# One decoder layer with product-key experts: looking up the chosen experts in two passes over packed payloads instead of three, and letting GpSimd split 16 table blocks first instead of 12

## What is computed

```
v1, i1 = lax.top_k(s1, K)          # 16 of 128 keys, first half of the query
v2, i2 = lax.top_k(s2, K)          # 16 of 128 keys, second half
cand = (v1[..., :, None] + v2[..., None, :]).reshape(TB, PEER_HEADS, K * K)
sc, ci = lax.top_k(cand, K)
idx = (jnp.take_along_axis(i1, ci // K, axis=-1) * PEER_N_KEYS
       + jnp.take_along_axis(i2, ci % K, axis=-1))
gate = jax.nn.softmax(sc.astype(jnp.float32), axis=-1)
act = jax.nn.gelu(jnp.einsum('thed,td->the', u_table[idx], xb).astype(jnp.float32), approximate=False)
return jnp.einsum('the,thed->td', (gate * act).astype(xb.dtype), v_table[idx])
```

## Time and profile before

| | us |
|---|---|
| median of 3 runs | 1542.87 |
| the profiled execution, its own time | 1549.56 |
| its span, first to last instruction | 1547.5 |
| PE busy | 1483.3 (96%) |
| DVE busy | 1184.3 (77%) |
| POOL busy | 674.9 (44%) |
| ACT busy | 641.2 (41%) |

### The profile page before, as it was taken

How to read it: one execution, slowest core, us unless ns; L and a number is a source line. 1 busy time by engine, 2 the same in 40 slices (tenths; PEclk the granted TensorE clock), 3 DMA queues, 4 the chain that set the end, 5 groups by cost and what they waited for, 6 DMA issues and landing times.

```text
span 1547.5 us, 23496 instructions
## 1 busy us (share of the span) xinstructions
PE 1483.3 (96%) x8069; PEld 1318.8 (85%) x8069; DVE 1184.3 (77%) x2357; ACT 641.2 (41%) x1058; POOL 674.9 (44%) x385
## 2 busy tenths in 40 slices
PE   6999889899999999999999999789999999999999
PEld 6879658788989998999999999768888888888887
DVE  4527473288999999878998899647787787787886
ACT  5363452222423433347777776332332322423321
POOL 2223141133558578864545544124334344343341
PEclk9999989999999999999999999989999999999999
DMA  5400202221559989999999999989999999999993
GB/s 200 143 28 1 109 1 72 82 82 59 169 201 325 332 286 309 381 370 341 351 361 367 358 378 372 365 299 351 354 352 349 347 354 349 351 345 348 354 348 124
DMA packets 186648, 412.68 MB, mean 267 GB/s; under 512 B 12980, under 2 KB 112564, under 8 KB 185048
## 3 DMA queue, kind: packets, MB, share of 16 engines
q1 hardware_dynamic: 144984, 260.87, 48.0%
q0 software_dynamic: 41600, 151.03, 25.9%
HBM read 361.37 MB, written 50.46 MB: 266 GB/s over the span
## 4 chain that ended last, share of the span: by engine, by line
PE 56%; DVE 25%; DMA 12%; issue 3%; POOL 3%; ACT 1%; SPq 1%; DVEq 0%; ACTq 0%
PE banks L1736 15%; PE banks L2011 11%; PE banks L2012 11%; PE banks L2013 11%; DMA u_rows<-in_u,idx 8%; DVE u_rows L1538 4%; DVE u_lo L1521 3%; DVE gate_rows L1593 3%; DMA u_raw<-in_uT 2%; DVE picked L1491 2%; POOL u_lo L715 2%; DVE picked L1486 2%; DVE e_f L1494 2%; PE banks L1943 1%; DVE oh L1589 1%
## 5 line engine op out<-in xcount | busy, mean ns | idle before, releaser
L763 POOL DMA_INDIRECT v_rows<-in_v,idx x128 | 202.8, 1584 | 341.7 <-DVE x_res L1673 295.9
L2011 PE MATMUL banks<-v_hi,w_hi 128*128 128x512 f32 x768 | 300.1, 391 | 7.2 <-DVE v_lo L1615 7.2
L2012 PE MATMUL banks<-v_lo,w_hi 128*128 128x512 f32 x768 | 299.9, 390 | 0.0
L2013 PE MATMUL banks<-v_hi,w_lo 128*128 128x512 f32 x768 | 299.7, 390 | 0.0
L731 POOL DMA_INDIRECT u_rows<-in_u,idx x160 | 205.4, 1284 | 154.0 <-DVE z L1538 108.1
L1088 ACT ACTIVATE v_hi<-v_raw 128x1024 fp32r<-128x1024 f32 x128 | 125.8, 1049 | 340.1 <-PE banks L2013 321.5
L1615 DVE TENSOR_TENSOR v_lo<-v_raw,v_hi 128x1024 fp32r<-128x1024 f32 x128 | 153.5, 1220 | 125.4 <-ACT v_hi L1088 125.4
L1943 PE MATMUL banks<-h_hi,u_lo 128*128 128x352 f32 x1024 | 189.9, 328 | 18.3 <-DVE u_lo L1521 11.4
L1943 PE MATMUL banks<-h_lo,u_hi 128*128 128x352 f32 x1024 | 198.2, 328 | 0.0
L715 POOL TENSOR_TENSOR u_lo<-u_raw,u_hi 128x1024 fp32r<-128x1024 f32 x64 | 159.4, 2493 | 84.1 <-DVE opened L1558 53.9
L1943 PE MATMUL banks<-h_hi,u_hi 128*128 128x352 f32 x1024 | 192.2, 330 | 3.2 <-ACT act_out L1012 3.2
(11 more groups left out here) (268 smaller groups left out, 2040.6 us busy)
## 6 DMA issues: line engine op xcount, KB each, us to landing
u_raw<-in_uT SPq DMA_DIRECT2D x128, 512.0 KB, 6.1
v_raw<-in_v SPq DMA_DIRECT2D x128, 512.0 KB, 6.0
gates<-gate_scratch SPq DMA_DIRECT2D x32, 768.0 KB, 12.4
act_scratch<-act_out SPq DMA_DIRECT2D x128, 176.0 KB, 4.6
gate_scratch<-stage SPq DMA_DIRECT2D x11, 2048.0 KB, 8.7
act_in<-act_scratch SPq DMA_DIRECT2D x32, 704.0 KB, 7.0
wi_raw<-in_w_in SPq DMA_DIRECT2D x8, 1024.0 KB, 8.6
wq_raw<-in_w_q SPq DMA_DIRECT2D x8, 1024.0 KB, 5.4
```

What stands on the lines that cost most here:

```text
L763: nc.gpsimd.indirect_dma_start(v_rows[s % V_ROWS][:], None, v_flat, bass.IndirectOffsetOnAxis(ap=idx0[:, s:s + 1], axis=0)).then_inc(vg_in ...
L2011: mm(y, w, v_hi[q][:, j, ds], start=first and j == 0, stop=False)
L2012: mm(y, w, v_lo[q][:, j, ds], start=False, stop=False)
L2013: end = mm(y, w_lo[q][:, j, t * P:(t + 1) * P], v_hi[q][:, j, ds], start=False, stop=last and j == GROUP - 1)
```

## The change

- **Two passes instead of three.** `pay` now carries the position too: before the layout, `PACK` = 32768 times the position at which the pair will stand is added to the two parts of the payload (one more DVE instruction of 256 elements in each `choose`, with a wait behind it), from a constant of 32 columns. The position found is multiplied by `PACK` when it is cast. The first pass subtracts the two, over the same 3200 elements; at the winner the difference is the expert's number, below 16384, elsewhere it is at least 16384 away from zero. The second pass takes the minimum of the absolute values. The copy `iota_c` (L1447) goes.
- **GpSimd splits 16 blocks first.** `POOL_FIRST` is 16, `SHARE_FROM` 20: POOL splits blocks 0 to 15 ahead of its gathers, DVE 16 to 19, and then they alternate.
- **Dots.** The "aa" at n = 14 and 16 go, since they stand two blocks ahead of POOL's shared blocks; four "a" come at n = 58, 62, 66 and 70. The number of dots in the lookup stage stays 71, that of all 160, and the gate stage's dots stay where they were.
- **Pieces.** `PIECE_SIZE` is 1800, the sizes follow the new pieces (25,100 for each `choose` instead of 31,400), and at each block the pieces are run ahead of `splits_and_dots(n)`, not behind it. They begin at n = 14 instead of n = 10.

```
-POOL_FIRST, SHARE_FROM = 12, 16
+POOL_FIRST, SHARE_FROM = 16, 20
...
-for _n in range(PRE + 32, POST):
+for _n in [*range(PRE - 14, PRE, 4), *range(PRE + 32, POST)]:
     DOTS[_n] += "a"
...
-PIECE_SIZE = 2150
-CHOOSE_SIZES = (400, 2000, 1000, 3100, 1000, 1900, 600, 3350, 3350, 3350, 3350, 3350, 3350, 200, 400, 700)
+PIECE_SIZE = 1800
+CHOOSE_SIZES = (400, 2400, 1000, 3100, 1000, 1900, 600, 3350, 3350, 3350, 3350, 200, 400, 700)
...
-            step(nc.vector.tensor_copy(iota_c[:], consts[:, C_IOTA:C_IOTA + CAND]))
...
+                settle()
+                step(nc.vector.tensor_tensor(pay_f[:], pay_f[:], bc(packed_at, 2, PH), ALU.add))
                 settle()
...
-                step(nc.vector.tensor_copy(sc_f[:], sc_i[:]))
+                step(nc.vector.tensor_scalar(sc_f[:], sc_i[:], PACK, None, ALU.mult))
...
-                    step(nc.vector.tensor_tensor(
-                        picked[:], bc(sc_f[:, hs, :], 3, CAND),
-                        bc(bc(iota_c[:], 1, TOPK), 1, PH // 2), ALU.is_equal))
+                    step(nc.vector.tensor_tensor(picked[:], bc(pay[:, hs, :], 2, TOPK), bc(sc_f[:, hs, :], 3, CAND),
+                                                 ALU.subtract))
                     yield
                     settle()
-                    step(nc.vector.tensor_tensor(picked[:], picked[:], bc(pay[:, hs, :], 2, TOPK), ALU.mult))
-                    yield
-                    settle()
-                    step(nc.vector.reduce_sum(e_f[:, hs, :], picked[:], axis=AX_X))
+                    step(nc.vector.tensor_reduce(e_f[:, hs, :], picked[:], AX_X, ALU.min,
+                                                 apply_absolute_value=True))
...
             for n in range(POOL_FIRST - 2, PRE):
-                splits_and_dots(n)
                 while done < (n - POOL_FIRST + 3) * PIECE_SIZE:
                     done += next(sizes)
                     next(work, None)
+                splits_and_dots(n)
...
+    first = np.array([at0 + (a - a0) * n for a0, na, n, at0 in RUNS for a in range(a0, a0 + na)])
+    at_pair = (PACK * np.concatenate([first, np.arange(TOPK)])).astype(np.float32)
```

More of the change, by code:

```diff
@@ L61 @@
 C_ID, C_IOTA, C_MIN, C_NEG, C_FREQ, C_GQ, C_GK = 0, 128, 256, 384, 512, 544, 736
-C_W = 928
+C_OFF = 928
+C_W = 960
+PACK = float(2**15)
 V_ATT, V_ML, V_CQ, V_CKV, V_BI, V_BF = 0, 8, 12, 14, 15, 16
@@ L208, in build @@
         gk = consts[:, C_GK:C_GK + DQK]
+        packed_at = consts[:, C_OFF:C_OFF + 2 * TOPK].rearrange("p (s a) -> p s a", s=2)
         c_raw = at("c_raw", 22, [P, KD, NW])
@@ L285, in build @@
         cand_tmp = at("cand_tmp", 95, [P, PH, CAND])
-        iota_c = at("iota_c", 96.75, [P, CAND])
         sc_i = at("sc_i", 97.5, [P, PH, TOPK], U32)
@@ L300, in build @@
         idx1 = at("idx1", 19.875, [P, NE], I32)
-        z1 = at("z1", 19.625, [P, NE])
+        z1 = at("z1", 203, [P, NE])
         z1t = at("z1t", 103.125, [P, NE])
@@ L2051 @@
         np.broadcast_to(inv_freq.astype(np.float32), (P, HALF)),
-        rows(q_norm_g), rows(k_norm_g)], axis=1)
+        rows(q_norm_g), rows(k_norm_g), rows(at_pair)], axis=1)
     head_rows = np.zeros((H, H, P), np.float32)
```

## The result

The changed kernel has a median of 1527.75 us (1522.25 to 1542.04, 15 runs), the one before 1542.87 us (1538.47 to 1547.04, 15 runs); the ratio is 0.9899 with a 95% interval of 0.988 to 0.9918, so it is faster by 1.0%, 15 to 16 us. 1529 was forecast. The sum behind that number held less well than the number, as the stages show: between the two profiled executions the gain is 1549.56 - 1528.92 = 20.6 us, where the sum has 14.25. The changed kernel's profiled execution took 1528.92 us.

A forecast was written before the change was run, and what follows sets the result against it. PE bounds the kernel, losing 21.4 us in the lookup stage to a late DVE, a full DVE, then full DMA engines. Terms -6.6 - 7.65 - 0 = -14.25 on the median 1542.87 give 1528.6, say 1529 us; range 1524 to 1538.

The forecast's parts named there:

- The start: `choose(0)` and block 12: shorter `choose(0)` and POOL's 16 first splits remove PE's wait and slow matmuls, -6.6 us.
- DVE from 459.6 to 627.25: Lookup stage: relieved DVE wins back 7.65 of 11.85 us, leaving 3 for uneven loading and 1.2 for the `idx1n` halt.
- What gets out of the way: In `choose`: eight long two-input passes go, freeing POOL at up to eight places by 3.1 us; no own term.
- The last 16 blocks: Lookup stage from 627.25 to 691.0 us: four more gathers offset by the old debt; 2.95 us lost stays.
- The debt: Last 16 blocks before: one to three late gathers caught up in 25 us, set against four gathers' 5.0 us.
- The gate stage, unchanged: Behind the lookup stage: dots and one-hot rows do not change, the stage moves whole, 5.76 us a block.
- The signs named beforehand: Changed profile: no wait at block 12, first gather 445 to 448, minimum 3.4 to 3.6, lookup end about 677 us.
- The sum onto the median: Whole kernel: the gain of 14.25 us, put on the median of 1542.87, gives 1528.6, say 1529 us.
- A: Lookup stage from block 47 on: DMA engines take over, losing 12 us; gain 8, 1535 us; chance 0.26.
- B: Lookup stage: DVE's lead and POOL's relief swallow the rest; residue 3 us, gain 18.4, 1524.5 us; chance 0.13.
- C: In `choose`: absolute minimum costs 6.95 us, only the start is won; gain 5 to 8, 1536 to 1538; chance 0.08.
- D: In `choose`: absolute minimum dear, a reduction of 9.6 us; kernel slower, 1551 us and more; chance 0.03.

The follow-up runs named there:

- e1: Changed kernel's two passes alone, with first splits, dots and order of pieces of the kernel before; 1524.19 us, ratio 0.9872 to the kernel before.
- e2: Kernel before, three passes kept, with the rest of the change (16 first splits, moved dots, pieces ahead of splits); 1541.25 us, ratio 0.999 to before.
- e5: Changed kernel with the absolute minimum done twice, as a piece of its own; 1531.65 us, ratio 0.9921 to the kernel before.
- e6: Changed kernel with the subtraction done twice and the minimum once; 1541.93 us, ratio 0.9983 to the kernel before.
- e11: Changed kernel run again unaltered, in the third group of runs; 1527.09 us, ratio 0.9891 to the kernel before.
- e3: Changed kernel run again unaltered, in the first group, for a second profile; 1523.36 us, ratio 0.9875 to the kernel before.
- e8: Changed kernel with all sixteen single dots of the gate stage moved into the lookup stage; 1533.99 us, ratio 0.9933 to the kernel before.
- e9: Changed kernel with four of the gate stage's single dots moved to lookup blocks 21, 27, 33, 39; 1524.0 us, ratio 0.9878 to the kernel before.
- e10: Changed kernel with eight gate-stage dots moved to lookup blocks 21 to 42, a repeat run; 1525.13 us, ratio 0.9882 to the kernel before.
- e12: The kernel of e1 with eight gate-stage dots moved to lookup blocks 21 to 42; 1530.52 us, ratio 0.9905 to the kernel before.

## Why the prediction was right, and which terms were mis-sized

*The start, -6.6 us: right.* 6.6 us in one profile of before and 5.5 in the other became 0.0. What was put down to GpSimd's 16 first splits needs only the shorter `choose(0)` (e1), and they alone do not shorten the run by more than its noise (e2).

*DVE from 459.6 to 627.25, 4.2 us left: mis-sized, 0.0 is left.* The relief was priced rightly: minimum 3478 ns, and subtraction 4028 ns, six of them at 24.2 us, the dear end of the stated 20.9 to 24.2. The packing add, 0.45 us in the sum, shows in e1 as

```profile
439.47 0.43 DVE L1455 TENSOR_TENSOR pay_f<-pay_f,consts 128x256 f32<-128x256 f32 x1
```

What was wrong is the 3 us left for uneven loading and the 1.2 for the `idx1n` halt. The halt is still there, 3.8 us in DMA, and PE does not feel it. The reason given for the loss was too simple as well: a DVE without idle time was called the cause, while PE's waits there name GpSimd's `u_lo` (6.9 us) and hardly DVE's (0.8 us), and a DVE just as full in e5 leaves PE at pace until block 55.

*What gets out of the way, no term: the term was missing.* GpSimd's lateness was taken as part of DVE's losses. With as many long passes on DVE (e5, e6) the form of the third pass is worth 10 us. The working had the row for it, a gather's issue of 4.03 us against 0.94, and the changed page shows it summed up: 160 issues fell from 205.4 to 189.8 us. The Trainium skill's page "SBUF — State Buffer", section "Who interferes with whom", says that on this chip a `tensor_reduce` never contends with GpSimd, and the runs agree: with a second minimum (e5) the mean issue is 1440 ns, in the changed kernel over the same stretch 1449. The same section's inference, that writing descriptors is not held up by a two-input `tensor_tensor`, does not carry over to the whole issue of a gather, which is held up in e6. Which part of the issue it is, the descriptors or another, no run tells.

*The last 16 blocks, 2.95 us left: mis-sized.* 1.0 is left, and that is PE's own work. The second profile of before shows the same 1.0, so the loss that was left standing was that execution's. The debt that was set against the four gathers was also overrated: 25 us are 6.6 blocks at PE's pace and 9.8 MB, not six and 9, so the 10.4 MB moved were about one gather more than needed. Nothing of the four gathers' 5.0 us came: the bound below, all hidden, is what the runs show.

*The gate stage, unchanged: right in the profile pair* (219.05 us for 38 blocks in both), but it varies between executions, below.

*The signs named beforehand.* No wait at block 12 and a clock of 1.00, the first gather at 444.96, the minimum at 3.48 us, and 5.76 us a block in the gate stage came as stated. The lookup stage ended at about 670 us and not 677, and no block near 44 was late. None of the signs of being wrong came: the rate from block 47 on is 346 and 398 GB/s with 1.1 us of waits for `u_raw` in all, and the step into the gate stage is 6.4 us as before.

*The sum onto the median.* The lookup stage gave 20.4 us between the two first profiles and 17.5 from the one nearer to the median, not 14.25. Between the two first profiled executions all of it arrives, 20.6 us, so there the sum is 6.4 us short. Between the medians 15.1 us arrive in this result, 15.3 in e11's group and 19.4 in e3's. What makes these differ was not isolated. Two parts vary from execution to execution of one kernel: the blocks from 110 to 127 take 94.8 and 91.8 us in the two profiles of before and 95.9, 97.0 and 92.0 in three of after, and the gate stage varies by 6.6 us, below. So the sum was 3 to 6 us too low for the stage, and that the median came within 1 us of 1529 is in part luck.

*The rivals.* A, the DMA engines, was near: with the sixteen dots moved, eight of them to blocks 48 to 68 (e8), the lookup stage loses 10.3 us. B's lookup stage came, and more, but its time, 1524.5, only in e3's group (1523.36). C and D fell with the minimum at 3.48 us.

## What to carry to other kernels

Count an event that comes once for each block in windows, and set it against PE's own pace: it says what a stage can give and where. Then read whom the bound engine waits for there: an engine without idle time need not be the late one. When work is removed from VectorE, price it by its form too: here a two-input pass held up the issue of GpSimd's gathers (1801 against 1440 ns in the mean) and grew itself, and a reduction over the same elements did neither. A stall removed at the head of a stage need not show in the whole time while the stage behind it still waits: of 5.5 to 6.6 us the medians of e2 keep 1.6, which is not clear of noise.

## What the runs showed that was not expected

The gate stage has two paces for the same instructions. In the changed kernel's second execution 38 blocks take 212.41 us instead of 219.05:

```profile
675.63:888.04 212.41, 16.92 (x38) 1.00 0.98 369
```

5.59 us a block against 5.76, with a granted clock of 1.00 in both and PE without a wait but for 0.2 us. The difference is in the matmuls' own spacing. The first line is from the first execution's timeline, the second from the second's, and the other groups of L1943 differ in the same way:

```profile
678.85 1.49 PE L1943 MATMUL banks<-h_hi,u_lo 128*128 128x352 f32 x8
```

```profile
773.11 1.43 PE L1943 MATMUL banks<-h_hi,u_lo 128*128 128x352 f32 x8
```

Which pace an execution takes does not follow the kernel: e2, e9 and e10 had the fast one (213.58, 211.96 and 212.28 us), e1, e5 to e8, e11 and e12 the slow one (219.05 to 219.65). The kernel before was slow in both profiles. Four early dots (e9, 1517.3 us in its profiled execution) and the eight of e10 (1516.94) have it in the execution with the lowest single time; that the pace explains those times was not tested further. It is worth 6.6 us, about half of the spread between single executions of one kernel (1536.36 to 1550.52 for the one before in e1's group). What sets it stays open; no run was made for it.
